# Two projection tiles of the last attention pass move from one pass to the next, with the embedding's product four steps on

## What is computed

```python
h = rms_norm(x, mix_norm_g)
dq, dk, dv, bq, bk, bv, z = jnp.split(h @ w_in, IN_SPLIT_IDX, axis=-1)
a = diff_attention(norm(dq), norm(dk), dv, lam, slopes)   # 4 heads of 2 x 64
b = dilated_attention(norm(bq), norm(bk), bv, slopes)     # 8 heads of 64
y = jnp.concatenate([a, b], axis=-1) * jax.nn.silu(z)
x = x + y @ w_out
gate = jax.nn.sigmoid(rms_norm(x, ple_norm_g) @ w_ple_gate)
return x + gate * (p @ w_ple_proj)                        # p: (1024, 256), the embedding
```

## Time and profile before

| | |
|---|---|
| median of 3 runs | 2986.96 us (2986.27 to 2989.28) |
| profiled execution | 2988.33 us, its span 2986.6 us |
| mean granted clock of TensorE | 0.977 |
| TensorE busy | 2832.6 us, 95% |
| VectorE busy | 1776.4 us, 59% |
| ScalarE busy | 1073.6 us, 36% |
| GpSimd busy | 907.1 us, 30% |
| adds of the eight mixer passes | 1999.0 to 2765.4 us |

### The profile page before, as it was taken

How to read it: one execution, slowest core, us unless ns; L and a number is a source line. 1 busy time by engine, 2 the same in 40 slices (tenths; PEclk the granted TensorE clock), 3 DMA queues, 4 the chain that set the end, 5 groups by cost and what they waited for, 6 DMA issues and landing times. The chain is left out here.

```text
span 2986.6 us, 39151 instructions
## 1 busy us (share of the span) xinstructions
PE 2832.6 (95%) x15342; PEld 2110.4 (71%) x15342; DVE 1776.4 (59%) x2635; ACT 1073.6 (36%) x1763; POOL 907.1 (30%) x531
## 2 busy tenths in 40 slices
PE   6999999999998999999999998879999999997898
PEld 5879797977876777777768876656666655553677
DVE  5787878784103344444452135767767777786486
ACT  4342525252101223332241013356666544343232
POOL 1233333333662211111113335432212222231365
PEclk8999999999998999999999999989999999999999
DMA  4132424135332111111113235310111011102534
GB/s 161 60 80 71 85 71 85 64 78 215 124 115 62 40 47 51 51 51 44 51 71 119 79 115 183 111 49 15 45 40 58 21 60 55 52 23 84 209 122 113
DMA packets 114085, 241.22 MB, mean 81 GB/s; under 512 B 8944, under 2 KB 52720, under 8 KB 113904
## 3 DMA queue, kind: packets, MB, share of 16 engines
q1 hardware_dynamic: 63648, 176.86, 18.2%
q10 hardware_dynamic: 50256, 61.87, 7.0%
HBM read 194.60 MB, written 44.11 MB: 80 GB/s over the span
## 5 line engine op out<-in xcount | busy, mean ns | idle before, releaser
L79 PE MATMUL psum<-u_h,w_hi 128*128 128x512 f32 (+2 forms) x2624 | 1008.0, 384 | 42.5 <-POOL w_lo L137 19.5
L80 PE MATMUL psum<-u_h,w_hi 128*128 128x512 f32 (+2 forms) x2624 | 968.6, 369 | 0.0
L81 PE MATMUL psum<-u_h,w_lo 128*128 128x512 f32 (+2 forms) x2624 | 966.9, 368 | 0.0
L135 POOL TENSOR_SCALAR w_hi<-w_raw 128x1024 fp32r<-128x1024 f32 x212 | 246.9, 1165 | 1520.4 <-ACTq L1324 519.9
L79 PEld LDWEIGHTS psum<-u_h,w_hi 128*128 128x128 f32 x2624 | 497.9, 190 | 185.7 <-issue 81.1
L137 POOL TENSOR_TENSOR w_lo<-w_raw,w_hi 128x1024 fp32r<-128x1024 f32 x212 | 545.4, 2573 | 17.7
L81 PEld LDWEIGHTS psum<-u_h,w_lo 128*128 128x128 f32 x2624 | 497.7, 190 | 71.8
L80 PEld LDWEIGHTS psum<-u_h,w_hi 128*128 128x128 f32 x2624 | 498.5, 190 | 67.0 <-issue 5.7
L2541 DVE TENSOR_TENSOR a_exp<-psum,a_strips 128x1024 f32<-128x1024 f32 x128 | 156.4, 1222 | 134.9 <-PE psum L2222 133.5
L2384 ACT ACTIVATE a_exp<-a_exp 128x1024 f32<-128x1024 f32 x128 | 135.5, 1059 | 243.9 <-DVE a_exp L2541 243.9
L1349 ACT ACTIVATE f_exp<-psum 128x1024 f32<-128x1024 f32 (+4 forms) x112 | 82.1, 734 | 193.0 <-PE psum L1207 94.0
(11 more groups left out here) (388 smaller groups left out, 4451.5 us busy)
## 6 DMA issues: line engine op xcount, KB each, us to landing
w_raw<-in_w_all SPq DMA_DIRECT2D x212, 512.0 KB, 3.6
sums_rows<-s_acs ACTq DMA_DIRECT2D x32, 512.0 KB, 8.5
a_strips<-in_strips SPq DMA_DIRECT2D x12, 960.0 KB, 7.1
f_decay<-s_nc SPq DMA_DIRECT2D x16, 520.0 KB, 5.5
s_y<-conv_out ACTq DMA_DIRECT2D x16, 512.0 KB, 3.0
yo_raw<-s_y ACTq DMA_DIRECT2D x8, 1024.0 KB, 9.5
x_tok<-in_x SPq DMA_DIRECT2D x8, 512.0 KB, 8.5
s_xT<-xT SPq DMA_DIRECT2D x8, 512.0 KB, 4.9
```

The source lines that it names most:

```text
L79: nc.tensor.matmul(out, w_hi[:, k], a_hi, start=(k == 0 and first), stop=False)
L80: nc.tensor.matmul(out, w_hi[:, k], a_lo, start=False, stop=False)
L81: return nc.tensor.matmul(out, w_lo[:, k], a_hi, start=False, stop=(k == kk - 1 and final))
L135: self.nc.gpsimd.tensor_scalar(self.hi[:, r], self.raw[:, r], 1.0, 1.0, ALU.mult, ALU.mult).then_inc(self.hi_done, 1)
```

## The change

`parts` gets a third list for q = 7: 48 units in the steps of pass 6 where 64 stood, and `share` gives the other 16, those of GZ0 and GZ1, to steps 0 to 3 of pass 7, four in each. `empty` and `gates` follow them, so that the SiLUs of pass 7 come at the end of its step 4 and not at the end of pass 6. The turns of the embedding go from steps 0 and 2 to 4 and 6, and its products from one a step (two in step 4) to two a step in steps 8 to 12 and one in 13 to 15. On GpSimd the split of the embedding's weight now waits for the last projection, and the split of output tile 37 (`W.split` with n = 35) goes from the head of pass 7 to behind it. On SP the embedding's loads wait for two projected tiles fewer.

```diff
-    parts = lambda q: [8, 8, 8, 8, 8, 3, 5, 4, 4, 4, 4, 0, 0, 0, 0, 0] if q == 0 else [5, 5, 5, 5, 4, 4, 4, 4, 4, 3, 3, 3, 3, 4, 4, 4]
+    parts = lambda q: [8, 8, 8, 8, 8, 3, 5, 4, 4, 4, 4, 0, 0, 0, 0, 0] if q == 0 else (
+        [5, 5, 5, 5, 4, 4, 4, 4, 4, 3, 3, 3, 3, 4, 4, 4] if q < PASSES - 1 else [5, 5, 5, 5, 4, 4, 4, 2, 2, 2, 2, 2, 2, 2, 1, 1])
...
     def share(q, x):
 
+        if q == PASSES:
+            return [(GZ0 + i // KT, i % KT) for i in range(4 * x, 4 * x + 4)] if x < 4 else []
         n = sum(parts(q)[:x])
...
-        TURN_AT, PLE_AT = {0: 0, 2: 1}, {x: [0, 1] if x == 4 else [x - 3] for x in range(4, U)}
+        TURN_AT, PLE_AT = {4: 0, 6: 1}, {x: [2 * x - 16, 2 * x - 15] if x <= 12 else [x - 3] for x in range(8, U)}
...
                 if p == LAST:
-                    sp.wait_ge(gfull, 8 * PASSES)
+                    sp.wait_ge(gfull, 8 * PASSES - 2)
...
-                    elif x == 0:
+                    elif x == 0 and p < LAST:
                         W.split(pool, 0, 0, 4 * p + 7)
...
             pool.wait_ge(w_got, 16)
+            pool.wait_ge(gfull, 8 * PASSES)
...
-            W.split(pool, 0, 0, 36)
+            for n in (35, 36):
+                W.split(pool, 0, 0, n)
...
-                    gemms = share(q, x) if q < PASSES else []
+                    gemms = share(q, x)
...
-                        project(q, g, k)
+                        project(min(q, LAST), g, k)
...
-                    for g, k in share(q, x) if q < PASSES else []:
+                    for g, k in share(q, x):
                         if k == KT - 1:
-                            empty(q, g)
+                            empty(min(q, LAST), g)
...
-                    if x == 15 and q < PASSES:
+                    if x == 15 and q < LAST:
                         gates(q)
+                    if p == LAST and x == 4:
+                        gates(LAST)
```

## The result

The changed kernel takes 3007.01 us (median of 4 runs, 3004.42 to 3007.96), the kernel before, run beside it, 2986.78 (four runs, one more than above): ratio 1.0064, 95% interval 1.005 to 1.0078, slower by 20.2 us. The prediction said 3005.0, range 2991 to 3013. The profiled execution took 3007.37 us, 19.0 more than that of before.

The account below looks back on a forecast made before the run. TensorE and VectorE take turns as the bound in pass 6, nothing is full in pass 7. −5.3 − 3.8 − 3.0 + 1.4 + 28.7 = +18.0 us on 2986.96 gives 3005 us, range 2991 to 3013.

Parts of the forecast that it names:

- Five waits in steps 9 to 13: Pass 7: TensorE's products wait 3 to 3.5 us for ScalarE's copies, held behind the exponential; +20.5 us before the clock.
- Their size: Steps 9 to 13 of pass 7, without clock loss: 25.7 + 8.1 + 6.7 = 40.5 us where 20.0 stood.
- The clock: Behind each of the five waits TensorE runs slow, 1.6 us lost each, +8.2 us; rival of clock kept, chance 0.21.
- Pass 6: Steps 7 to 15, which lose 16 projection units: −5.3 us, nothing from steps 8 to 12, where VectorE sets the round.
- Steps 0 to 3: Pass 7, with four projection units added in each step: 22.6 us for 26.4, −3.8 us.
- Steps 4 to 7: Pass 7, with the gates and the embedding's turns: −3.0 us with contention and slow clock, −5.7 without.
- Blocked sums: VectorE's sums over steps 3 to 5 of pass 7 stand behind GpSimd's weight split: 0 to 2.9 us, taken as 2.0.
- The chain through the gates: Pass 7: the gates at the end of step 4 delay step 5's exponential; next add 10.15 us after step 4's.
- Step 8: Pass 7, row-sum product and two embedding products: 6.0 us, 1.0 more with the clock down, 5.6 before; +0.4 to +1.4.
- The upper bound of the prediction: Whole kernel with all contention and clock loss: +25.5 us, 3012.5 us.
- the add of (7,4): VectorE's score add at step 4 of pass 7, a sign: some 9 us earlier than 2714.9.
- The tables: ScalarE's two table switches for the SiLUs: priced by the rows, no drain; rival by the page, 3008 us, chance 0.03.

Follow-up runs that it names:

- e1: The changed kernel with ScalarE's copies of the embedding's products put ahead of the exponential of the same step; 2981.6 us (0.9979).
- e2: The changed kernel with one embedding product in each of steps 8 to 15 of pass 7, the other eight behind the last step; 2985.46 us (0.9987).
- e4: The kernel before with only the new places of the embedding's turns and products, projections, gates and queues as before; 3008.99 us (1.0067).
- e3: The changed kernel with 14 throwaway matmuls (12 in steps 12 and 13) ahead of the first product of steps 9 to 13 of pass 7; 2998.89 us (1.003).
- e7: e1 with the two SiLUs and table loads of pass 7 at the end of step 3, not 4; 2981.84 us (0.9981).
- e11: e9 with the gates back at the end of step 4; 2979.52 us (0.997).
- e9: e8 with GpSimd's split of output tile 37 held back until VectorE has made the embedding's low parts; 2978.25 us (0.997).
- e10: e4 with the copies ahead of the exponential, that is e1 without the moved projections, gates and queues; 2985.26 us (0.9984).
- e6: e1 with GpSimd's split of the embedding's weight in four slices of 512 columns in place of one pass over 2048; 2980.24 us (0.9973).
- e8: e6 and e7 together: e1 with the sliced weight split and the gates at the end of step 3; 2982.90 us (0.9984).

## Why the prediction was right

**Place and mechanism.** Five waits in steps 9 to 13, each ended by ScalarE's copy, three of 3.4 us and two of 2.9: as read from the earlier trace rows. e1 removes them by order alone, e2 by placing one product a step, e4 brings them back without anything else of the change.

**Their size.** Forecast 40.5 us for the five rounds without the clock, measured 40.4 in e3.

**The clock.** Forecast five times 1.6, paid four times, 6.3 us for 8.2: 26.8 us in the stretch for 28.7. That an idle time of the same length cost 1.6 us once and nothing another time (step 13 here, step 11 in e4) means that a single event was a fair price but a count of them is not certain by one or two. The rule of the Trainium skill that was weighed, a drop in every turn of a waiting loop ("TensorE: Matmul & The Clock Gate", HAM oscillation), held in four of five turns.

**Pass 6.** −5.7 for −5.3: steps 8 to 12 gave back 0.2 of six units (4.1 us of TensorE's work), as VectorE's rows had it; steps 7, 13, 14 and 15 gave 1.4, 1.4, 0.4 and 2.3.

**Steps 0 to 3** were under-priced by 1.3 us: step 0 took 6.49 for 6.1, and round (7,3) 6.17 for 5.3, as the first blocked sum fell there and not in the next stretch.

**Steps 4 to 7** came out at 21.9 as forecast, by errors that cancel. Blocked sums cost 1.6 in rounds 4 and 5 (with 0.9 in round 3, 2.5 in all for the 2.0 taken), and round 6 came out 1.3 over its 4.15, for the 0.7 that were taken for the clock. The chain through the gates (10.15 us) was not what set rounds 4 and 5 in the changed kernel, as e7 shows; only in e11, with GpSimd's long passes out of the way, do the two rounds come to 3.73 + 6.62 = 10.35.

**Step 8** took 7.43 us for 7.0: the step itself was a little shorter than the 6.0 taken, 5.84 in e4 and e9, where the granted clock was 1.00, and the slow clock cost 1.6 and not 1.0. In all of these runs TensorE stands 2.3 us ahead of the row-sum product there; the clock fell behind it in the changed kernel, e1, e2, e3, e7 and e10, and not in e4, e6, e8, e9 and e11.

**The total.** The terms missed by −0.4, +1.3, 0, +0.4 and −1.9, which leaves −0.6: the sum of 17.4 for 18.0 is closer than its parts. The measured time is 2 us above the forecast: these −0.6, the 1.7 us ahead of the stretch, which no term held, and some 1 us by which the medians lie further apart (20.2 us) than the profiled executions (19.0). The upper bound of the prediction doesn't follow from its terms: −5.3 − 3.8 − 2.1 + 1.4 + 20.5 + 13, with −2.1 from −5.7 + 2.9 + 0.7, is +23.7 (3010.7 us) and not +25.5. And of its signs one came out otherwise, the add of (7,4), 6.5 us earlier than 2714.9 and not 9: 1.7 by that same start, 1.3 by steps 0 to 3, less 0.4 for pass 6.

**The tables.** The earlier trace rows against the drain of 1.38 us that the Trainium skill states ("ScalarE: Activation LUTs", What ACT_TABLE_LOAD costs): the changed kernel has the load at 2710.75, the SiLU at 2712.04, the second load 0.01 us behind the SiLUs, and the first stands 0.03 us behind the exponential ahead of it. No drain is seen, and the rows were the right price.

Left open: why a given wait loses the clock and another of the same length doesn't (steps 12 and 13, and step 8 from run to run), and the 1.7 us ahead of the stretch, which vary from run to run in untouched code.

## What to carry to other kernels

When two results a step go through two buffers, ask where in the emptying engine's own order the emptying stands: behind an instruction that depends on this step's product, it puts the whole chain (here scores, add, exponential, copy) between the producer and its next start. Look for the one place in the old trace where the new pattern already occurs; its duration, times the new count, was here worth more than any sum of busy times. Work taken from a step pays only if its engine sets that step: six of sixteen units moved from steps that VectorE set brought 0.2 us.

## What the hardware showed beyond that

A sum or difference of two SBUF tiles on VectorE that starts while a GpSimd pass runs does not overlap with it: in the five cases shown here (the three sums after the change, the mixer part in e8) it ends as long after the end of the GpSimd pass as it takes alone, less 0.14 us (1.08 of 1.22, 0.54 of 0.68). The GpSimd instruction of 5.44 us cost VectorE 1.9 us in the one sum that stood behind it; the other two sums stood behind other passes. Cutting it into slices brought 0.9 us in round (7,3), and round (7,5) became shorter only in e9, where the next long pass was moved too. TensorE kept 2.4 GHz through a wait when it was fed matmuls whose results nobody reads: 6.3 us in the stretch for 66 such matmuls.
